# Long convolutions of a diffusion trunk layer: even frequencies folded twice, the first order's folding moved into the projections

## The reference, cut to what matters

```python
def long_conv(u, k_f, bias):
    length = u.shape[1]
    uf = u.astype(jnp.float32)
    y = jnp.fft.irfft(jnp.fft.rfft(uf, n=2 * length, axis=1) * k_f[None], n=2 * length, axis=1)[:, :length]
    return y + uf * bias.astype(jnp.float32)

def hyena_mixer(u, conv_w, conv_b, k_f, hy_bias):
    uc = short_conv(u, conv_w, conv_b)          # three taps per channel
    v, x1, x2 = jnp.split(uc, 3, axis=-1)
    z = x1.astype(jnp.float32) * long_conv(v, k_f[:, 0], hy_bias[0])     # first order
    y = x2.astype(jnp.float32) * long_conv(z, k_f[:, 1], hy_bias[1])     # second order
    return y.astype(u.dtype)
```

## Time and profile before

| | us |
|---|---|
| median of 3 runs | 3388.33 (3383.38 to 3390.08) |
| the profiled execution, own time | 3388.24 |
| its span, first to last instruction | 3386.5 |
| of it, the phase `hyena` | about 212 |

### The profile page before, as it was taken

One profiled execution on the slowest core, in us unless ns is written; L12 is line 12 of the kernel. 1 busy time (PEld: TensorE's weight loads), 2 busy tenths in 40 slices (PEclk: granted clock), 3 DMA queues, 4 the chain that ended last, 5 costly groups with the idle time before them and its releaser, 6 DMA issues.

```text
span 3386.5 us, 54111 instructions
## 1 busy us (share of the span) xinstructions
PE 3194.2 (94%) x22270; PEld 2430.6 (72%) x22270; DVE 2191.4 (65%) x2815; ACT 1655.8 (49%) x2156; POOL 382.8 (11%) x319
## 2 busy tenths in 40 slices
PE   5997999979899894999999999999999999999997
PEld 2443888878778773777777777777777777777775
DVE  7644233167666547777777777777777777777767
ACT  1103222156411323666666666666666666666665
POOL 2210100011244131000000000000000000000010
PEclk8998999989999896999999999999999999999999
DMA  5464432254676434788778777777777778777786
GB/s 175 170 228 177 116 115 84 73 143 127 230 245 216 149 100 162 278 297 295 272 288 294 274 288 292 275 288 290 274 290 292 275 287 295 270 289 294 275 316 247
DMA packets 226035, 791.14 MB, mean 234 GB/s; under 512 B 28526, under 2 KB 35322, under 8 KB 221565
## 3 DMA queue, kind: packets, MB, share of 16 engines
q1 hardware_dynamic: 206028, 722.02, 57.6%
q0 software_dynamic: 19760, 65.65, 6.8%
HBM read 730.31 MB, written 57.26 MB: 233 GB/s over the span
## 4 chain that ended last, share of the span: by engine, by line
PE 58%; DVE 1%; DMA 1%; ACT 0%; issue 0%; POOL 0%; SPq 0%; ACTq 0%; POOLq 0%; DVEq 0%
PE exp_bank L2806 15%; PE exp_bank L2808 14%; PE exp_bank L2807 14%; PE exp_bank L2816 14%; PE exp_bank L2788 1%; DMA exp_xb<-residual 1%; PE exp_bank L2790 1%; PE exp_bank L2774 0%; DMA out_y<-exp_xb 0%; DVE exp_lo L2500 0%; DVE g_pick L2367 0%; DVE g_pick L2366 0%; DVE g_pick L2369 0%; DVE exp_xb L2714 0%; DMA exp_xq<-hidden_rows,g_rows_q 0%
## 5 line engine op out<-in xcount | busy, mean ns | idle before, releaser
L2500 DVE TENSOR_TENSOR exp_lo<-exp_raw,exp_hi 128x1024 fp32r<-128x1024 f32 x1056 | 1277.8, 1223 | 249.7 <-ACT exp_hi L2496 190.8
L2496 ACT ACTIVATE exp_hi<-exp_raw 128x1024 fp32r<-128x1024 f32 x1056 | 1119.1, 1061 | 570.8 <-PE exp_bank L2808 556.7
L2806 PE MATMUL exp_bank<-exp_hi,exp_xt 128*128 128x512 f32 (+1 forms) x1536 | 588.6, 383 | 1.3 <-DVE exp_xt L2655 1.0
L2808 PE MATMUL exp_bank<-exp_hi,exp_xt 128*128 128x512 f32 (+1 forms) x1536 | 572.0, 372 | 0.0
L2807 PE MATMUL exp_bank<-exp_lo,exp_xt 128*128 128x512 f32 (+1 forms) x1536 | 571.7, 372 | 0.0
L2806 PEld LDWEIGHTS exp_bank<-exp_hi,exp_xt 128*128 128x128 f32 x1536 | 289.6, 189 | 87.0 <-issue 39.1
L2808 PEld LDWEIGHTS exp_bank<-exp_hi,exp_xt 128*128 128x128 f32 x1536 | 289.7, 189 | 51.9
L2816 PE MATMUL exp_bank<-exp_raw,exp_xtp 128*32 128x256 f32 (+1 forms) x6144 | 324.1, 363 | 0.0
L2807 PEld LDWEIGHTS exp_bank<-exp_lo,exp_xt 128*128 128x128 f32 x1536 | 290.2, 189 | 45.4
L2806 PE MATMUL exp_bank<-exp_hi,exp_hid 128*128 128x512 f32 x704 | 282.8, 402 | 0.7 <-DVE exp_lo L2500 0.7
L2816 PEld LDWEIGHTS exp_bank<-exp_raw,exp_xtp 128*32 128x32 f32 x6144 | 185.1, 110 | 127.0 <-issue 30.8
(11 more groups left out here) (413 smaller groups left out, 4299.1 us busy)
## 6 DMA issues: line engine op xcount, KB each, us to landing
exp_raw<-in_w SPq DMA_DIRECT2D x1056, 512.0 KB
hy_table<-in_basis_s POOLq DMA_DIRECT2D x64, 512.0 KB
carry_tiles<-in_w_ada SPq DMA_DIRECT2D x24, 1024.0 KB, 5.5
proj_raw<-in_w_in SPq DMA_DIRECT2D x24, 512.0 KB
filt_table<-in_kbasis_s SPq DMA_DIRECT2D x18, 512.0 KB, 6.1
spectrum_s<-filt_spec SPq DMA_DIRECT2D x34, 256.0 KB, 2.2
carry_flex<-spectrum_s SPq DMA_DIRECT2D x16, 512.0 KB
features<-proj_xr SPq DMA_DIRECT2D x12, 512.0 KB, 3.0
```

What stands on the lines that cost most here:

```text
L2496: act.activation(st.hi[:, n % st.ns, :], raw(n), ACT.Copy).then_inc(st.hi_done, 1)
L2500: dve.tensor_tensor(st.lo[:, n % st.ns, :], raw(n), st.hi[:, n % st.ns, :].bitcast(F32), ALU.subtract).then_inc(st.lo_done, 1)
L2806: pe.matmul(out, xh, wh, start=(k == 0), stop=False)
L2808: mm = pe.matmul(out, xl, wh, start=False, stop=(k == nk - 1))
```

## The change

The sums and differences of the even frequencies are folded a second time, at 256 positions. A cosine of an even frequency is itself symmetric or antisymmetric there, according to whether half the frequency is even or odd, so each forward bank of steps 0 to 3 needs 2 tiles of positions and not 4: 12 matmuls to a step. The frequencies of these four steps are sorted anew for it, so SP loads the spectrum of each in two DMAs of 64 partitions, every other row. The odd frequencies keep 24 matmuls; their tables are built for twice-folded input. In the inverse the even frequencies give only 256 columns each (half the columns), into one or the other half of the far banks, and the new `unfold` makes the 512 positions of the even half of them; `even` now starts with steps 4 and 5. The chunks of the tables go from 16 to 13 an order. The second folding of the first order, with the first one, is made in the projection (`folded`) on the four blocks of `v`; the second order's is in `fold_s`. `products`, `combine`, `high`, `low` and `out_s` keep their instructions.

```diff
+            def folded(x, out):
+                half, hp = TS // 2, TP // 2
+                dve.wait_ge(s_cv, cv(x) + 2)
+                up, down = out[:, TP + 1:TP + 1 + half], out[:, T:TP + half:-1]
+                dve.tensor_tensor(pad[:, TP + 2:TP + 2 + half], up, down, ALU.add)
+                dve.tensor_tensor(pad[:, TP + 2 + half:T + 2], up, down, ALU.subtract)
+                up, down = out[:, 0:hp], out[:, TP - 1:hp - 1:-1]
+                dve.tensor_tensor(pad[:, 1:hp + 1], up, down, ALU.add)
+                dve.tensor_tensor(pad[:, hp + 1:TP + 1], up, down, ALU.subtract).then_inc(s_cv, 1)
+                dve.wait_ge(s_cv, cv(x) + 3)
+                once = pad[:, TP + 2:T + 2].rearrange("p (s x) -> p s x", s=2)
+                twice = out[:, TP + 1:T + 1].rearrange("p (s x) -> p s x", s=2)
+                near, far = once[:, :, 0:half // 2], once[:, :, half - 1:half // 2 - 1:-1]
+                dve.tensor_tensor(twice[:, :, 0:half // 2], near, far, ALU.add)
+                dve.tensor_tensor(twice[:, :, half // 2:half], near, far, ALU.subtract)
+                dve.tensor_copy(out[:, 0:TP], pad[:, 1:TP + 1]).then_inc(s_cv, 1)
...
+                    if x < 4:
+                        folded(x, out)

         @block.tensor
...
 def hyena(nc, a, g, carry):


-    M, MT, NJ, NC = TS // 2, TS // 256, TS // 128, 16
-    MP = TP // 2
-    NS = 5
+    M, MT, NJ, NC = TS // 2, TS // 256, TS // 128, 13
...
         def used(o, c):
-            return o * NC + c
+            return o * SO + c
+
+        def freed(c):
+            return c // NC * SO + FREE[c % NC]
+
+        def forward_at(j):
+
+            return (j // 2, j % 2 * 4) if j < MT else (j - 2, 0)
+
+        def blocks(j, kind):
+
+            return [2 * ((j // 2 + kind) % 2) + t for t in range(2)] if j < MT else range(MT)
...
+                o, j = divmod(n, STEPS)
+                if j >= MT:
+                    sp.dma_start(kt[:, n % 2, :, :], spectrum(n)[0:2].rearrange("a p f -> p a f")).then_inc(s_kt[n % 2], 16)
+                else:
+                    for t in range(2):
+                        k = g["Ks"][o, 2 * (j % 2) + t, 0:2, j // 2::2, :]
+                        sp.dma_start(kt[64 * t:64 * t + 64, n % 2, :, :], k.rearrange("a p f -> p a f")).then_inc(s_kt[n % 2], 16)
...
-                    pool.wait_ge(s_step, c - NS + 1)
+                    pool.wait_ge(s_step, freed(c - NS))
...
-                    load(c0 + NS + j)
-                load(c0 + 13)
-                load(c0 + 14)
+                    if j in (1, 3, 4, 5, 6, 7):
+                        load(c0 + NS + (1, 3, 4, 5, 6, 7).index(j))
+                load(c0 + 11)
                 combine(o * STEPS + NJ)
                 combine(o * STEPS + NJ + 1)
-                load(c0 + 15)
...
-                    act.activation(half(ct), far(o, ct)[:], ACT.Copy).then_inc(s_pc, 1)
+                    act.activation(half(ct)[:, 0:M2], far(o, ct)[:, 0:M2], ACT.Copy).then_inc(s_pc, 1)
...
-                dve.tensor_tensor(fold[:, ct, TP + M:T], up, down, ALU.subtract).then_inc(s_fold, 1)
+                dve.tensor_tensor(fold[:, ct, TP + M:T], up, down, ALU.subtract).then_inc(s_f1, 1)
+                dve.wait_ge(s_f1, ct + 1)
+                once, twice = (x[:, ct, TP:T].rearrange("p (s x) -> p s x", s=2) for x in (fold, u))
+                up, down = once[:, :, 0:M2], once[:, :, M - 1:M2 - 1:-1]
+                dve.tensor_tensor(twice[:, :, 0:M2], up, down, ALU.add)
+                dve.tensor_tensor(twice[:, :, M2:M], up, down, ALU.subtract).then_inc(s_fold, 1)
...
+            def unfold(o, ct):
+                dve.wait_ge(s_pc, 4 * o + ct + 1)
+                e = half(ct)
+                dve.tensor_tensor(e[:, M - 1:M2 - 1:-1], e[:, 0:M2], far(o, ct)[:, M2:M], ALU.subtract)
+                dve.tensor_tensor(e[:, 0:M2], e[:, 0:M2], far(o, ct)[:, M2:M], ALU.add).then_inc(s_e, 1)
+
             def out_s(o, ct):
-                dve.wait_ge(s_pc, 4 * o + ct + 1)
+                dve.wait_ge(s_e, 4 * o + ct + 1)
...
             dve.wait_ge(carry.s_u, 16)
-            for ct in range(4):
-                fold_s(ct)
-            fold_p()
...
                 for ct in range(4):
+                    unfold(o, ct)
+                for ct in range(4):
...
-                    pe.wait_ge(s_fold, 4 * o + s + 1)
+                    if o:
+                        pe.wait_ge(s_fold, s + 1)
+                    elif s == 0:
+                        pe.wait_ge(carry.s_u, 16)
                     if o and s == 0:
-                        pe.wait_ge(s_pc, 4)
+                        pe.wait_ge(s_e, 4)
...
+                ready(pe, o * NC + c)
...
                     out = near(o, j % 2 * 2 + kind)
-                    for t in range(MT):
+                    ts = blocks(j, kind)
+                    for t in ts:
...
+                        pe.matmul(out[:], bh, uh[:, src, t, :], start=(t == ts[0]), stop=False)
                         pe.matmul(out[:], bh, ul[:, src, t, :], start=False, stop=False)
-                        mm = pe.matmul(out[:], bl, uh[:, src, t, :], start=False, stop=(t == MT - 1))
+                        mm = pe.matmul(out[:], bl, uh[:, src, t, :], start=False, stop=(t == ts[-1]))
+                        x += 1
                 mm.then_inc(s_step, 1)
...
             def even(o, i):
-                ready(pe, o * NC + 8 + i)
-                for j in (2 * i, 2 * i + 1):
+                c = o * NC + (6, 7, 7, 8)[i]
+                ready(pe, c)
+                for j in EVEN[i]:
                     pe.wait_ge(s_Pl, 2 * (o * NJ + j) + 2)
                     for ct in range(4):
-                        mm = inverse(o, far(o, ct), ct, j, j // MT, 16 + j)
+                        if j < MT:
+                            mm = inverse(far(o, ct)[:, j // 2 * M2:(j // 2 + 1) * M2], ct, j, 0, c, j, M2, False)
+                        else:
+                            mm = inverse(far(o, ct)[:], ct, j, 1, c, j % 2, M, j == EVEN[0][0])
                 mm.then_inc(s_step, 1)
...
             def prompt_transposes(o):
-                pe.wait_ge(s_foldp, o + 1)
+                if o:
+                    pe.wait_ge(s_foldp, 1)
```

More of the change, by code:

```diff
@@ L1550, in spectrum, with k_landed, edge_landed @@
             return g["Ks"][o, j] if j < NJ else g["Kp"][o, j - NJ]
-        def edges(n):
-            return 2 * (n // STEPS) + (1 if n % STEPS > NJ else 0)
+        def k_landed(n):
+            return 16 * sum(2 if m % STEPS < MT else 1 for m in range(n % 2, n + 1, 2))
+        def edge_landed(n):
+            return 48 * (n // STEPS) + (32 if n % STEPS == 0 else 48)
         def gates(o, c0, c1):
@@ L1788, in forward @@
                     out = near(o, j % 2 * 2 + kind)
-                    for t in range(MT):
+                    ts = blocks(j, kind)
+                    for t in ts:
                         if j == 0:
                             pe.wait_ge(s_ul, o * 2 * MT + src * MT + t + 1)
-                        bh, bl = tile(0, o * NC + j, kind * MT + t), tile(1, o * NC + j, kind * MT + t)
-                        pe.matmul(out[:], bh, uh[:, src, t, :], start=(t == 0), stop=False)
+                        bh, bl = tile(0, o * NC + c, x), tile(1, o * NC + c, x)
+                        pe.matmul(out[:], bh, uh[:, src, t, :], start=(t == ts[0]), stop=False)
@@ L1794, in forward, with inverse @@
                         pe.matmul(out[:], bh, ul[:, src, t, :], start=False, stop=False)
-                        mm = pe.matmul(out[:], bl, uh[:, src, t, :], start=False, stop=(t == MT - 1))
+                        mm = pe.matmul(out[:], bl, uh[:, src, t, :], start=False, stop=(t == ts[-1]))
+                        x += 1
                 mm.then_inc(s_step, 1)
-            def inverse(o, out, ct, j, kind, x):
-                c = o * NC + x // 2
-                bh, bl = tile(0, c, x % 2, M), tile(1, c, x % 2, M)
+            def inverse(out, ct, j, kind, c, x, w, first):
+                bh, bl = tile(0, c, x, w), tile(1, c, x, w)
@@ L1801, in inverse @@
                 xh, xl = Ph[:, kind, j, ct * 128:(ct + 1) * 128], Pl[:, kind, j, ct * 128:(ct + 1) * 128]
-                pe.matmul(out[:], xh, bh, start=(j == 0), stop=False)
-                pe.matmul(out[:], xh, bl, start=False, stop=False)
-                return pe.matmul(out[:], xl, bh, start=False, stop=(j == NJ - 1))
+                pe.matmul(out, xh, bh, start=first, stop=False)
+                pe.matmul(out, xh, bl, start=False, stop=False)
+                return pe.matmul(out, xl, bh, start=False, stop=(j == NJ - 1))
@@ L1828, in prompt_transposes @@
                     for ct in range(4):
-                        tr = pe.transpose(near(o, x)[:, ct * 128:(ct + 1) * 128], fold[:, ct, x * MP:(x + 1) * MP], g["ident"][:])
+                        tr = pe.transpose(near(o, x)[:, ct * 128:(ct + 1) * 128], (fold if o else u)[:, ct, x * MP:(x + 1) * MP],
+                                          g["ident"][:])
```

(18 more changed lines are left out.)

48 lines of the change are left out of this document (29 added, 19 removed).

## The result

| | us, median | lowest to highest | runs |
|---|---|---|---|
| before | 3384.53 | 3383.14 to 3391.57 | 8 |
| after | 3394.43 | 3391.85 to 3400.53 | 8 |

The ratio is 1.0029, 95% interval [1.0020, 1.0037]: some 10 us lost, where 2.7 were forecast. The profiled execution of the changed kernel is the slowest of its eight (3400.53 us, span 3398.7), so the profile shows more than the median: 12.3 us over the profiled one of before.

The account below looks back on a forecast made before the run. A loop of DVE and POOL, 6.06 us a forward step, was taken as the bound; 1.3 us gained and 4.0 lost to TensorE's clock made +2.7 on 3388.24, so 3390.9 us, range 3381 to 3399.

Parts of the forecast that it names:

- the wait for the spectrum at step 2: Sign of being wrong: in the forward stage, DVE's products wait for the spectrum's DMA at steps 2 or 3.
- The loop, not PE, set the stage: Forward stage: DVE-POOL loop of 6.06 us a step, not PE's 5.44, sets pace; opposite rival 6 in 100, 3356 us.
- The second products: Second group of forward products: 5.2 us behind the first, no longer 5.44; gain 0.24 us in each order.
- From P to X: From start of last forward products (P) to end of prompt's inverse (X), 26.35 us before: gain 0.4 us.
- The out stage: First order's output tiles: four `unfold` and the second folding on DVE; loss 3.2 us, bounds 2.6 and 3.6.
- The end of the second order: Second order's output: `unfold` takes more than DVE's idle ahead of `out_s(0)`; loss 1.0 us, bounds 0 and 2.2.
- The projection: `folded` adds about 3.7 us of DVE, hidden by idle time: nothing; rival of too small cover 3 in 100, 3405.7 us.
- The third: Third group of first-order products: its spectrum lands earlier; gain 1.2 us, bounds 0 and 1.2.
- SP* issues 10 DMAs more: SP's DMA queue: 10 more DMAs at 0.4 us each, with nothing late in the queue; cost nothing.
- the spectrum comes late: Rival, 7 in 100: the spectrum of steps 2 and 3 lands late, four times 2.4 us; 3400.5 us.
- The start: First order's first products: at 905.2 instead of 907.49; gain 2.3 us, bounds 0 and 2.9.
- The clock: TensorE's half clock after idle gaps: loss 4.0 us, bounds 0 and 7.4; rival at every gap 12 in 100, 3394.3 us.

## Why the prediction held, and where it did not

The measured loss is 9.9 us where 2.7 were forecast: inside the range, with the right sign, 7.2 us more than the sum had. That it stayed inside is in part luck: the range was drawn for the clock and for small terms, and one term alone was off by 8.3 us. The profiled execution, 12.3 us slower than that of before, lies outside, at 3400.53 us. Of the prediction's own signs of being wrong one came, the wait for the spectrum at step 2, and `hyena` was not within 3 us of its old length but 12 us longer.

**What held.** *The loop, not PE, set the stage.* The distance stayed at 6.06, PE stood idle between steps, 32 us of saved matmul work were worth nothing, and once the loop was loosened 12.6 of them appeared. What the prediction did not see is how close the two were: with the loop loosened and nothing folded, PE set the end of each order, and only 2.7 us were gained. *The second products*: 5.24 us behind the first, forecast 5.2. *From P to X*: stalls of 2.60 and 2.02 us for 2.8 and 1.9 forecast; the stretch is 27.68 us, which is 26.35 + 1.74 of clock - 0.4. *The out stage*: +2.5 for 3.2, since `unfold` took 2.65 us, near the lower bound, and a tile 5.24. *The end of the second order*: 0, its lower bound, for 1.0. *The projection*: nothing.

**What failed.** The step "*The third* waited for the spectrum's DMA until 920.21 [...] I take the landing to be earlier: gain 1.2, bounds 0 and 1.2" and with it "*SP* issues 10 DMAs more, 0.4 us each [...] in a queue with nothing late. Nothing." The queue did have something late: the third spectrum, in the earlier trace rows. In place of the gain of 1.2 stands a loss of 7.1 us (14.34 - 7.28), so the term was off by 8.3 of the 9.6 us that the profile lies above the forecast. The bounds excluded a loss because only the bytes and the issues were counted, not the shape. The rival "the spectrum comes late" had the mechanism right, and the argument set against it there ("the same bytes") was wrong; but it spread the loss over four groups, and it fell on one. The second order's groups show no wait for the spectrum, though its halves are the same. There POOL issued the table's loads from 1002.99 on, 12.7 us ahead of the first forward matmul (1015.66), where the first order had 8.4 us (894.05 to 902.48), and the queues moved only 212 GB/s at a share of 0.60 from 1018 to 1030; that this is why was not tried apart.

**The start** gained 0.4 us for 2.3. PE waited 2.47 us for the table's first chunk (902.48), but this explains little: 12 matmuls from there at full clock, 902.48 + 12 x 0.2267 + 0.2, allow products at 905.4. They came at 907.08, and the 1.7 us between are the half clock behind that wait. The prediction priced the clock at the other gaps and left this one out. It is no chance of one execution: in the seven other profiles of kernels with the change the first products come 4.6 to 4.7 us behind the first forward matmul, not 2.9. The halved DMAs did not make the chunk late, since with one DMA it landed no sooner; why it lands 0.4 to 1.4 us later behind the phase's start than before, in all eight profiles, is open.

**The clock** cost 1.7 + 1.74 + 3.05 = 6.5 us in the profile for 4.0 forecast, and not where forecast: 1.7 at the start (forecast 0), 0 at the first order's forward, 1.74 at the inverse (forecast 0), 3.05 at the second order's forward (forecast 1.6), and the 0.8 at the last transposes was hidden. The stall of 2.60 us was followed by full clock once and by half clock once. In another execution, that of the changed kernel with the gates late, the first order's forward took 5.17 us and its inverse 5.47: the place is no constant of the kernel. The full price is up to 3.1 us, because all 8 instructions ran at half clock, not "3.2 us at half clock lose half".

What stays open: what part of the slowness of two DMAs of 64 partitions is the ports' and what part the number of DMAs', and how much of the third group's delay each execution has; the median's 9.9 us are less than the profile's 12.3.

## What to carry to other kernels

Before an engine's saved work is counted, find which release sets the distance of its steps; here two waits had to be made finer before 48 matmuls less in each order counted for anything. Two rows of work can be nearly equal, as the loop's and PE's were here: shortening one alone then gives almost nothing, and the idle time of the other (here 0.25 us ahead of `prompt_forward`) is the sign of it. A change that reads data in another pattern changes its DMAs: count their partitions and what stands ahead of them in the queue, above all where the trace of before already shows one landing late. If a tile is needed in an interleaved order, change the layout in DRAM so that one DMA of 128 partitions still brings it.

## What the chip did that was not expected

Splitting a load of 128 partitions into two of 64, both in flight, lowered the core's whole DMA rate over 12 us from 406 to 339 GB/s in the kernel before and, against one DMA, from 375 to 299 in the changed one (all from 4.4 to 4.8 us behind the start of the phase), and made other queues' packets dearer as well (44 to 55 us of engine time for a MB of table). The granted clock after idle stretches of equal length (2.60 us) was at full level in one order and at half in the other of the same execution.
